# A conformer convolution on four engines: eight products for GpSimd, 19 taps for VectorE, and a weight chunk's low part in two halves

## The reference

```python
def conformer_conv(h, w_pw1, b_pw1, w_dw, b_dw, ln_g, ln_b, w_pw2, b_pw2):
    u = h @ w_pw1 + b_pw1
    a, gate = jnp.split(u, 2, axis=-1)
    u = a * jax.nn.sigmoid(gate)
    u = jnp.pad(u, ((0, 0), (CONV_WIDTH - 1, 0), (0, 0)))
    u = lax.conv_general_dilated(u, w_dw[:, None, :], window_strides=(1,), padding='VALID',
                                 dimension_numbers=('NWC', 'WIO', 'NWC'),
                                 feature_group_count=D_MODEL) + b_dw
    u = jax.nn.silu(layer_norm(u, ln_g, ln_b))
    return u @ w_pw2 + b_pw2
```

## Time and profile before

| | |
|---|---|
| median of 3 runs | 1974.17 us (1973.81 to 1974.92) |
| the profiled execution | 1972.33 us, its span 1970.5 us |
| TensorE busy | 1922.2 us, 98% of the span |
| VectorE, ScalarE, GpSimd busy | 826.4, 776.3, 670.8 us |
| granted TensorE clock | 0.998 |

### The profile page before, as it was taken

The page is one execution under the profiler, slowest core; times in us unless marked ns, Lnnn a source line. Parts: engine busy times, 40 slices in busy tenths (PEclk is TensorE's granted clock), DMA queues, the critical chain, the costliest instruction groups (busy, mean ns, idle before and its releaser), DMA issues.

```text
span 1970.5 us, 25009 instructions
## 1 busy us (share of the span) xinstructions
PE 1922.2 (98%) x9890; PEld 1594.3 (81%) x9890; DVE 826.4 (42%) x1368; ACT 776.3 (39%) x1162; POOL 670.8 (34%) x208
## 2 busy tenths in 40 slices
PE   6998999999999999999999999999999999999999
PEld 4665988888897768888888897778888898888887
DVE  6996721111266363611111377756552342112122
ACT  6565432222345452523222256754454342222221
POOL 2884044434301300244343313222122403434442
PEclk9999999999999999999999999999999999999999
DMA  5111264222221301322222212111113323222222
GB/s 189 65 43 65 69 127 94 107 86 106 89 88 49 123 1 43 107 107 86 107 97 94 107 55 86 65 49 60 44 60 112 107 86 107 87 106 85 107 80 91
DMA packets 30366, 169.40 MB, mean 86 GB/s; under 512 B 3739, under 2 KB 6076, under 8 KB 13372
## 3 DMA queue, kind: packets, MB, share of 16 engines
q1 hardware_dynamic: 30268, 168.01, 25.4%
HBM read 162.22 MB, written 5.77 MB: 85 GB/s over the span
## 4 chain that ended last, share of the span: by engine, by line
PE 90%; DVE 4%; ACT 3%; POOL 1%; issue 1%; DMA 0%; SPq 0%; DVEq 0%; POOLq 0%; ACTq 0%
PE ps L2043 62%; PE ps L2064 8%; PE ps L2397 4%; PE ps L2463 3%; PE ps L2155 1%; ACT whi L591 1%; PE ps L2557 1%; PE ps L2126 1%; POOL wlo L502 1%; PE ps L2575 1%; PE ps L2304 1%; PE ps L2303 1%; DVE wlo L1241 1%; PE ps L2321 1%; PE ps L2286 1%
## 5 line engine op out<-in xcount | busy, mean ns | idle before, releaser
L502 POOL TENSOR_TENSOR wlo<-wraw,whi 128x2048 fp32r<-128x2048 f32 (+5 forms) x142 | 588.6, 4145 | 1271.6 <-ACT whi L591 1271.6
L591 ACT ACTIVATE whi<-wraw 128x2048 fp32r<-128x2048 f32 (+4 forms) x160 | 279.5, 1747 | 373.3 <-PE ps L2043 349.9
L2043 PE MATMUL ps<-xh,whi 128*128 128x512 f32 x1044 | 413.4, 396 | 4.8 <-DVE xl L1221 3.7
L2043 PE MATMUL ps<-xl,whi 128*128 128x512 f32 x1044 | 406.9, 390 | 0.0
L2043 PE MATMUL ps<-xh,wlo 128*128 128x512 f32 x1044 | 406.8, 390 | 0.0
L2043 PE MATMUL ps<-hh,whi 128*128 128x512 f32 x752 | 295.6, 393 | 6.2 <-DVE hl L1481 6.0
L2043 PE MATMUL ps<-hh,wlo 128*128 128x512 f32 x752 | 293.4, 390 | 0.0
L2043 PE MATMUL ps<-hl,whi 128*128 128x512 f32 x752 | 293.3, 390 | 0.0
L2043 PEld LDWEIGHTS ps<-xh,whi 128*128 128x128 f32 x1044 | 196.3, 188 | 51.3 <-issue 9.9
L2043 PEld LDWEIGHTS ps<-xl,whi 128*128 128x128 f32 x1044 | 196.4, 188 | 43.2 <-issue 3.1
L2043 PEld LDWEIGHTS ps<-xh,wlo 128*128 128x128 f32 x1044 | 196.2, 188 | 41.0
(11 more groups left out here) (334 smaller groups left out, 2831.7 us busy)
## 6 DMA issues: line engine op xcount, KB each, us to landing
wraw<-stream SPq DMA_DIRECT2D x132, 1024.0 KB, 4.8
wraw<-stream SPq DMA_DIRECT2D x12, 768.0 KB, 4.2
wraw<-stream SPq DMA_DIRECT2D x6, 384.0 KB, 3.2
resid<-x SPq DMA_DIRECT2D x4, 512.0 KB, 5.2
wraw<-stream SPq DMA_DIRECT2D x8, 256.0 KB, 3.2
branch_scratch<-RS SPq DMA_DIRECT2D x8, 256.0 KB, 2.0
wraw<-stream SPq DMA_DIRECT2D x4, 512.0 KB, 3.7
out<-resid SPq DMA_DIRECT2D x4, 512.0 KB, 2.6
```

The source lines that it names most:

```text
L502: pool.tensor_tensor(wlo[:, p, 0:w], wraw[:, p, 0:w], whi[:, p, 0:w], ALU.subtract).then_inc(lo_ready, 1)
L591: act.activation(whi[:, p, 0:w], wraw[:, p, 0:w], ACT.Copy).then_inc(hi_ready, 1)
L2043: ins = pe.matmul(ps[:, bank + n, :], wt[:, p, w], xt[:, k0 + k, :], start=k == 0 and q == 0, stop=k == k_tiles - 1 and q == 2)
```

## The change

GpSimd adds eight products in place of seven for tiles 0 to 6 (`POOL_TAPS` 8) and seven as before for tile 7 (`POOL_LAST` 7). VectorE has 19 taps for tiles 0 to 6, an even chain of ten and an odd chain of nine, and 15 for tile 7 as before. In `middle` the pair is turned round: the even chain's tap comes first and the odd chain's tap second. GpSimd's low part of chunks 2 to 8 is done in two halves of 128x1024: the first ahead of the additions, and the second, which raises `lo_ready`, behind them. For chunk 8 the second half comes behind all additions and shifts, just ahead of chunk 9's low part.

```diff
-PE_TAPS, POOL_TAPS = 4, 7
+PE_TAPS, POOL_TAPS, POOL_LAST = 4, 8, 7
...
-HALF_CHAIN = DVE_TAPS // 4
+EVENS, ODDS = (DVE_TAPS + 1) // 2, DVE_TAPS // 2
...
+            def rest_half(c, half, h=0):
+                p, w = c % 2, slice(half * CW // 2, (half + 1) * CW // 2)
+                if half == 0:
+                    pool.wait_ge(hi_ready, h * 2 + (c + 1))
+                    pool.wait_ge(chunk_done, h * 2 + (c - 1))
+                ins = pool.tensor_tensor(wlo[:, p, w], wraw[:, p, w], whi[:, p, w], ALU.subtract)
+                if half:
+                    ins.then_inc(lo_ready, 1)
+
-            def add_products(j, h=0):
-                for i in range(1, POOL_TAPS):
+            def add_products(j, h=0, n=POOL_TAPS):
+                for i in range(1, n):
...
             with pool.Fori(1, DT // 2 - 1) as h:
                 for j in range(2):
-                    rest(2 + j, h)
+                    rest_half(2 + j, 0, h)
                     add_products(j, h)
+                    rest_half(2 + j, 1, h)
...
-            rest(DT)
+            rest_half(DT, 0)
             add_products(DT - 2)
...
-            add_products(DT - 1)
+            add_products(DT - 1, n=POOL_LAST)
...
             for j in range(3, DT - 1):
                 shift(j)
+            rest_half(DT, 1)
             rest(DT + 1)
...
             def middle(j, h, n, first, last):
                 for m in range(first, last):
-                    tap_add(j, h, 1, m, n + (2 * m - 1))
-                    tap_add(j, h, 0, HALF_CHAIN + m, n + 2 * m)
+                    tap_add(j, h, 0, EVENS // 2 + m, n + max(2 * m - 1, 0))
+                    if m < ODDS - EVENS // 2:
+                        tap_add(j, h, 1, m, n + 2 * m)
```

More of the change, by code:

```diff
@@ L513, in _ @@
             pool.wait_ge(lo_ready, 2)
[L514 to L517, removed]
+            for j in range(2):
+                rest_half(2 + j, 0)
+                add_products(j)
+                rest_half(2 + j, 1)
             with pool.Fori(1, DT // 2 - 1) as h:
                 for j in range(2):
-                    rest(2 + j, h)
+                    rest_half(2 + j, 0, h)
                     add_products(j, h)
+                    rest_half(2 + j, 1, h)
             def shift(j):
@@ L532, in _ @@
                 shift(j)
-            add_products(DT - 1)
-            pool.wait_ge(products_added, DT * (POOL_TAPS - 1))
+            add_products(DT - 1, n=POOL_LAST)
+            pool.wait_ge(products_added, (DT - 1) * (POOL_TAPS - 1) + POOL_LAST - 1)
             pool.tensor_tensor(pool_sum[1], pool_sum[1], RS[:, :], ALU.subtract).then_inc(products_shifted, 1)
@@ L737, in sigmoid, with conv_products @@
                                bias=bias_).then_inc(gate_ready, 1)
-            def conv_products(j, h=0):
+            def conv_products(j, h=0, n=POOL_TAPS):
                 gated(act, j, h)
-                for i in range(POOL_TAPS):
+                for i in range(n):
                     if i >= 4:
@@ L753, in _ @@
             for i in range(LAST_TAPS):
-                act.activation(last_diag[i], ident, ACT.Copy, scale=tap(PE_TAPS + POOL_TAPS + i, 1, DT // 2 - 1))
+                act.activation(last_diag[i], ident, ACT.Copy, scale=tap(PE_TAPS + POOL_LAST + i, 1, DT // 2 - 1))
             sigmoid(0)
@@ L774, in _ @@
                 head(c0 + j + DT)
-                conv_products(j, DT // 2 - 1)
+                conv_products(j, DT // 2 - 1, POOL_LAST if j else POOL_TAPS)
             root_table()
@@ L1418, in end_and_begin @@
             def end_and_begin(j, h, n):
-                for m in range(HALF_CHAIN):
-                    tap_add(j - 1, h, 1, HALF_CHAIN + m, n + (2 * m - 1))
+                for m in range(EVENS // 2):
+                    tap_add(j - 1, h, 1, ODDS - EVENS // 2 + m, n + (2 * m - 1))
                     tap_add(j, h, 0, m, n + 2 * m)
-                tile_sum(j - 1, h, n + (2 * HALF_CHAIN - 1))
+                tile_sum(j - 1, h, n + EVENS - 1)
             def middle(j, h, n, first, last):
                 for m in range(first, last):
-                    tap_add(j, h, 1, m, n + (2 * m - 1))
-                    tap_add(j, h, 0, HALF_CHAIN + m, n + 2 * m)
+                    tap_add(j, h, 0, EVENS // 2 + m, n + max(2 * m - 1, 0))
+                    if m < ODDS - EVENS // 2:
+                        tap_add(j, h, 1, m, n + 2 * m)
             gate(0)
-            evens = 2 * HALF_CHAIN - 1
-            for m in range(evens):
+            for m in range(EVENS - 1):
                 tap_add(0, 0, 0, m, m)
             gate(1)
[L1434 to L1437, removed]
+            begun = EVENS + ODDS - EVENS // 2
+            for m in range(ODDS - EVENS // 2):
+                tap_add(0, 0, 1, m, EVENS - 1 + m)
+            tap_add(0, 0, 0, EVENS - 1, EVENS - 1)
             with dve.Fori(0, DT // 2 - 1) as h:
@@ L1441, in _ @@
                     end_and_begin(j, h, n)
-                    middle(j, h, n + 2 * HALF_CHAIN, 0, 1)
+                    middle(j, h, n + EVENS, 0, 1)
                     gate(j + 1, h)
-                    middle(j, h, n + 2 * HALF_CHAIN, 1, HALF_CHAIN)
-            j, h, left = 1, DT // 2 - 1, DVE_TAPS - LAST_TAPS
+                    middle(j, h, n + EVENS, 1, EVENS // 2)
+            j, h, left = 1, DT // 2 - 1, TAPS - PE_TAPS - POOL_LAST - LAST_TAPS
             n = begun + (DT - 2) * DVE_TAPS
-            for m in range(HALF_CHAIN):
-                tap_add(0, h, 1, HALF_CHAIN + m, n + m - (m == 0))
-            n += HALF_CHAIN
+            for m in range(EVENS // 2):
+                tap_add(0, h, 1, ODDS - EVENS // 2 + m, n + m - (m == 0))
+            n += EVENS // 2
             tile_sum(0, h, n)
@@ L2152, in taps @@
                 weights = [(k, diag[at][k]) for k in range(PE_TAPS)]
-                weights += [(PE_TAPS + POOL_TAPS + i, last_diag[i]) for i in range(more)]
+                weights += [(PE_TAPS + POOL_LAST + i, last_diag[i]) for i in range(more)]
                 for n, (k, w) in enumerate(weights):
```

## The result

| | before | changed |
|---|---|---|
| median | 1973.43 us (6 runs, 1971.60 to 1974.92) | 1983.02 us (6 runs, 1981.62 to 1984.84) |
| profiled execution, span | 1972.33, 1970.5 us | 1983.07, 1981.3 us |
| second sigmoid to last sigmoid | 90.30 us | 98.46 us |
| last sigmoid to first pw2 matmul | 33.89 us | 33.74 us |

The changed kernel is slower: the ratio is 1.0052, 95% interval 1.0040 to 1.0063, or 7.9 to 12.4 us. The median is also above the main case's own range, to 1982.4, and next to the 1983.2 of the rival in which the clock falls once. The two lines at the foot of the table are the yardstick for all that follows.

What follows compares the result with a forecast made beforehand. TensorE, busy for 98% of the span, was taken to bound the kernel. The late low part added 7.1 us on the profiled 1972.3, or 7.0 on the median 1974.2, the other terms 0: 1981.2 us, range 1978.6 to 1984.0.

Steps and rivals of the forecast that it cites:

- main case: Whole kernel: low part late, 1981.2 us, own range 1980.2 to 1982.4, chance 0.68.
- the rival in which the clock falls once: TensorE at the first hole of 3.9 us: one fall to 1.2 GHz loses 2.0 us, 1983.2 us; chance 0.11.
- The late second half: Convolution stage, GpSimd: low part completes behind the additions, 2.5 us after TensorE would want it.
- T + 17.1: Low part of chunk j+2 ready 17.1 us after tile j's sigmoid T(j), not 7.2; TensorE wants it at 14.6.
- Its price: Last sigmoid of the convolution stage 7.1 us later through the loop over GpSimd; bounds 6.3 and 7.7.
- The first hole: TensorE ahead of chunk 2: low part ready at 49.7 us, wanted at 45.8, a hole of 3.9 us.
- The end of the stage: Behind the last sigmoid: shifts still fit, first pw2 matmul stays 33.9 us after it, cost 0.
- The port: VectorE's tap on GpSimd's sum stretches to about 3 us in every tile, hidden by 2.7 us before TensorE's taps.
- The clock: TensorE's clock falling to 1.2 GHz behind the first hole: a rival costing 2.0 us, chance 0.11.
- VectorE as the bound: Rival in the convolution stage: port time makes VectorE 16.3 us a tile, 2.2 us more, 1983.4 us; chance 0.09.

Runs made afterwards that it cites:

- undivided run: Changed kernel with the low part undivided and ahead of the additions, eight products and VectorE's order kept: 1982.69 us, ratio 1.0051 to the kernel before.
- The run again: The changed kernel once more, no edit: 1984.57 us, ratio 1.0058 to the kernel before.
- run with TensorE by halves: Changed kernel, but TensorE starts a chunk on the low part's first half and waits for the second behind its taps: 1976.36 us, ratio 1.0016.
- run with the second half in the middle: Changed kernel with the low part's second half between the third and the fourth addition: 1982.38 us, ratio 1.0057 to the kernel before.

## Why the prediction came out right, and what it missed

**The late second half**: shown. The low part lies at T + 16.8 for three of the chunks 4 to 7 in each profile and at T + 17.2 for the fourth, forecast T + 17.1. Letting TensorE wait by halves takes two thirds of the loss away with nothing else changed, and halves alone, with seven products, cost what the same sum gives for them.

**Its price**: 6.6 us, within the bounds 6.3 to 7.7. The first hole was 3.2 and 3.7 us in the two profiles for 3.9, because TensorE came to it 0.7 to 0.8 us later than in the profile before.

**The end of the stage**: 33.74 us from the last sigmoid to the first pw2 matmul, forecast 33.9. The moved half of chunk 8 and the second low part behind it cost nothing.

**The port**: hidden in the change, as argued. The tap took 0.75 to 2.69 us in the first profile rather than about 3 in every tile: 2.27 to 2.69 where it began with the second half or soon behind it (at 48.01, 79.28 and 112.55 us), 1.44 and 1.30 where it came in the middle of it (63.83 and 128.70), and 0.75 where it came behind it (97.03). The Trainium skill, "SBUF — State Buffer", section "Who interferes with whom", calls it an exclusive lock for the whole instruction, and the 5.06 and 3.91 us of the undivided run agree.

**The clock**: this term was mis-sized, and it is the one that failed. The prediction put nothing for it in the sum and gave it a chance of 0.11, once, behind the first hole only. It fell in the stage in both profiles of the change, and costs 1.6 and 4.2 us there. Four holes in place of one are four chances, and the rows of before had no hole between 2.68 and 5.97 us to judge by. The two profiled executions lie 10.8 us apart in span: 0.7 by the place of the second sigmoid, 8.2 in the stage (6.6 the loop, 1.6 the clock), 0.2 less behind it, 0.7 on the way to 573 us that no row explains, 1.3 at 750 us, and 0.1 after that. The medians lie 9.6 and 11.9 us apart in the two comparisons. How often the clock falls in the executions without a profile is not known, so that the medians can't be added up in the same way. The range was met because it was wide enough for one fall of the clock. The run again, whose profile has two in the stage, lies outside it, so there was some luck in it.

**VectorE as the bound** did not come about in the change: TensorE never waited for gate before the last taps in either profile.

## What to carry to other kernels

When work is moved behind other work on an engine, ask who waits for its completion and when: the second half of a weight chunk was put behind 9.5 us of additions, and TensorE, which needs it before anything of the sum, stood for it in four tiles. If a wait must be moved, split it where the consumer needs the parts, not only where the producer makes them. And an instruction on which another engine hangs should not queue behind one that itself waits: `gate` one place earlier closed the 2.93 us hole at tile 2, which one tap fewer on VectorE had not.

## What the runs showed of the hardware that was not expected

TensorE's clock fell behind holes of 1.83, 2.06, 2.23, 2.93, 3.24, 3.35, 3.70, 4.79 and 7.15 us, and did not behind others of 1.83, 2.12, 2.27, 2.67, 2.68 and 3.19. Of the holes of 2.42 us ahead of the sums of the layer norm it fell in that of the run with TensorE by halves, and did not behind that of the run with seven products and halves around the additions. So the length of one hole does not settle it. It fell while TensorE still stood in the holes of 3.70 and 7.15 us, but in the changed kernel when TensorE had already been back at work at full speed for 0.9 us. The Trainium skill, "TensorE: Matmul & The Clock Gate", Part 1, says that the state follows how busy TensorE has been of late, and these rows, in which no single length decides, do not speak against it. A hole of 2 us must be counted at its length plus the chance of a fall, which cost 1.5 to 2.6 us each time in the middle of the stage.

The lock between VectorE and GpSimd works both ways. In the undivided run a tap that had started at 100.60 made the subtraction behind it longer, 5.06 us for 4.57, and in the run with the second half in the middle a half begun at 98.98, behind a tap at 98.92, took 2.91 us for 2.36:

```profile
100.60 0.76 DVE L1412 SCALAR_TENSOR_TENSOR ps<-Z,PV,E 128x512 f32<-128x512 f32 x1 [2.70 <-POOL E L519]
```

```profile
100.69 5.06 POOL L502 TENSOR_TENSOR wlo<-wraw,whi 128x2048 fp32r<-128x2048 f32 x1 [0.28 <-ACT whi L599]
```
